# Moving steps of four engines' hand-written order in a fused two-layer encoder kernel

## The reference

```python
def encoder_layer(x, ...):
    hn = rmsnorm(x, g_pre_mix)
    proj = hn @ w_in                       # 1024 -> 3072
    # three token mixers on column groups of proj: dilated attention (q, k, v of 6 heads),
    # 2-D neighbourhood attention (4 heads), short gated convolution (384 channels)
    mixed = concat([y_dil, y_na, y_conv]) @ w_out
    x = x + rmsnorm(mixed, g_post_mix)
    hf = rmsnorm(x, g_pre_ffn)
    f = (silu(hf @ w_gate) * (hf @ w_up)) @ w_down      # 1024 -> 2816 -> 1024
    return x + rmsnorm(f, g_post_ffn)
# rmsnorm(x, g) = x * rsqrt(mean(x * x) + eps) * g
```

## Time and profile before

| | us |
|---|---|
| three runs, median | 3261.06 (3260.49 to 3262.88) |
| profiled execution, own time | 3261.06 |
| its span, first to last instruction | 3259.3 |
| TensorE busy | 3194.7 (98%) |
| VectorE busy | 1508.6 (46%) |
| ScalarE busy | 936.4 (29%) |
| GpSimd busy | 917.5 (28%) |
| mean granted TensorE clock | 0.993 of full speed |

### The profile page before, as it was taken

The page is one execution under the profiler, slowest core; times in us unless marked ns, Lnnn a source line. Parts: engine busy times, 40 slices in busy tenths (PEclk is TensorE's granted clock), DMA queues, the critical chain, the costliest instruction groups (busy, mean ns, idle before and its releaser), DMA issues.

```text
span 3259.3 us, 42970 instructions
## 1 busy us (share of the span) xinstructions
PE 3194.7 (98%) x17564; PEld 2726.9 (84%) x17564; DVE 1508.6 (46%) x3067; ACT 936.4 (29%) x1814; POOL 917.5 (28%) x653
## 2 busy tenths in 40 slices
PE   9999999999999999999999999999999999999997
PEld 8888887888888888888788888878888888888886
DVE  6766657253333333323687666562523333333336
ACT  5433444341111111111344344444411111111112
POOL 2111113553222222222342121135622222222223
PEclk9999999999999999999999999999999999999998
DMA  3111002131111111111321110121211111111112
GB/s 145 51 50 49 28 28 85 75 130 52 40 39 39 40 38 34 40 39 33 135 81 43 52 47 29 46 90 71 110 58 39 33 39 39 39 39 39 40 52 104
DMA packets 50483, 184.29 MB, mean 57 GB/s; under 512 B 8048, under 2 KB 11760, under 8 KB 46832
## 3 DMA queue, kind: packets, MB, share of 16 engines
q1 hardware_dynamic: 47984, 173.68, 15.7%
q10 hardware_dynamic: 2304, 7.87, 0.6%
HBM read 144.81 MB, written 28.84 MB: 53 GB/s over the span
## 4 chain that ended last, share of the span: by engine, by line
PE 88%; DVE 8%; issue 1%; ACT 1%; DMA 1%; POOL 0%; SPq 0%; DVEq 0%; POOLq 0%; ACTq 0%
PE PS L1783 26%; PE PS L1785 26%; PE PS L1784 25%; PE PS L1935 3%; PE PS L1904 3%; PE PS L1919 2%; DVE PT L1544 1%; DVE XL L1379 1%; DVE ACC L1372 1%; DVE ACC L1375 1%; PE PS L1820 1%; DVE YO L1375 1%; DVE YO L1372 1%; PE PS L1879 0%; ACT PT L1087 0%
## 5 line engine op out<-in xcount | busy, mean ns | idle before, releaser
L1783 PE MATMUL PS<-XH,WH 128*128 128x512 f32 (+1 forms) x3648 | 1325.7, 363 | 14.8 <-DVE XL L1379 4.4
L1785 PE MATMUL PS<-XH,WL 128*128 128x512 f32 (+1 forms) x3648 | 1299.9, 356 | 0.0
L1784 PE MATMUL PS<-XL,WH 128*128 128x512 f32 (+1 forms) x3648 | 1298.9, 356 | 0.0
L1783 PEld LDWEIGHTS PS<-XH,WH 128*128 128x128 f32 x3648 | 692.3, 190 | 138.9 <-issue 21.2
L1785 PEld LDWEIGHTS PS<-XH,WL 128*128 128x128 f32 x3648 | 692.3, 190 | 100.7
L1784 PEld LDWEIGHTS PS<-XL,WH 128*128 128x128 f32 x3648 | 692.9, 190 | 92.0
L808 POOL TENSOR_TENSOR WL<-RAW,WH 128x1024 fp32r<-128x1024 f32 x193 | 460.8, 2407 | 367.8 <-ACT WH L987 362.8
L831 POOL TENSOR_TENSOR SG<-SG,RS 128x512 f32<-128x512 f32 x132 | 147.2, 1115 | 994.5 <-ACT SG L1126 994.5
L1614 DVE TENSOR_TENSOR ACC<-ACC,PS 128x512 f32<-128x512 f32 (+1 forms) x480 | 286.4, 599 | 246.6 <-PE PS L1785 245.4
L1783 PE MATMUL PS<-HH,WH 128*128 128x512 f32 (+1 forms) x1056 | 379.3, 359 | 5.4 <-DVE ACC L1614 3.1
L1785 PE MATMUL PS<-HH,WL 128*128 128x512 f32 (+1 forms) x1056 | 378.9, 359 | 0.0
(11 more groups left out here) (123 smaller groups left out, 3019.5 us busy)
## 6 DMA issues: line engine op xcount, KB each, us to landing
RAW<-w_in SPq DMA_DIRECT2D x48, 512.0 KB, 3.5
RAW<-w_gate SPq DMA_DIRECT2D x44, 512.0 KB, 3.4
RAW<-w_up SPq DMA_DIRECT2D x44, 512.0 KB, 3.5
RAW<-w_down SPq DMA_DIRECT2D x44, 512.0 KB, 3.8
X<-parked SPq DMA_DIRECT2D x6, 2048.0 KB, 7.3
RAW<-w_out SPq DMA_DIRECT2D x16, 512.0 KB, 4.4
parked<-YO SPq DMA_DIRECT2D x4, 2048.0 KB, 6.6
mixed<-YB ACTq DMA_DIRECT2D x8, 640.0 KB, 2.9
```

The costliest lines, as they stand in the source:

```text
L1783: nc.tensor.matmul(out, wh, xh, start=first, stop=False)
L1784: nc.tensor.matmul(out, wh, xl, start=False, stop=False)
L1785: return nc.tensor.matmul(out, wl, xh, start=False, stop=last)
```

## The change

It moves instructions within the orders of four engines and adds or removes none:

- ScalarE, start: the high parts of the second and third weight (q, v) are made after the sixth and the eighth `first_high` of chunk 0 instead of both after the eighth.
- TensorE, start of layer 0: the sum of the input's chunk 1 is taken in the middle of the group q1 instead of after it.
- FFN stage 0, both layers: VectorE does all steps of chunk 2 before `hidden(L, 0, 0)` and `gate(L, 1, 0)`; ScalarE does all `new_high` of chunk 2 before `hidden_high(L, 0, 0)` and `silu(L, 1, 0)`, and `hidden_high(L, 0, 1)` goes between the sixth and the seventh square of chunk 2; GpSimd does `scaled_gate(L, 0, 1)` after the fifth tile's add (k = 4) of chunk 2 instead of after all.
- FFN last stage: VectorE puts three steps of chunk 0 (k = 3, 4, 5), not two (3, 4), between the accumulations of down chunk 1; it does no step of chunk 1 before `hidden(L, f + 1, 2)` (three or two before), and in the last layer four of them before the accumulations of down chunk 2. ScalarE follows with its `new_high` in layer 0.

```diff
@@ gpsimd
                 scaled_gate(L, 1, 0)
-                for k in range(KT):
+                for k in range(5):
                     add(e, "x", 2, k)
                 scaled_gate(L, 0, 1)
+                for k in range(5, KT):
+                    add(e, "x", 2, k)
                 invert(e, "x", 2)
@@ scalar
             for k in range(KT):
                 first_high(0, k)
-            high((0, "q", 0))
-            high((0, "v", 0))
+                if k in (5, 7):
+                    high((0, "q" if k == 5 else "v", 0))
...
                         square_new(e, 1, squared)
                         squared += 1
-                    if k == 4:
-                        hidden_high(L, 0, 0)
-                        silu(L, 1, 0)
+                hidden_high(L, 0, 0)
+                silu(L, 1, 0)
                 mean(e, "x", 1)
                 hidden_high(L, 1, 0)
                 keep(e, "x", 1)
                 for k in range(3):
                     square_new(e, 2, k)
                 silu(L, 0, 1)
-                for k in range(3, KT):
+                for k in range(3, 6):
                     square_new(e, 2, k)
                 hidden_high(L, 0, 1)
+                for k in range(6, KT):
+                    square_new(e, 2, k)
...
                 for k in range(KT):
                     square_acc(L, 1, k)
-                    if more_layers and k in (1, 4):
-                        new_high(e, 0, 3 + k // 4)
+                    if more_layers and k in (1, 3, 5):
+                        new_high(e, 0, 3 + k // 2)
...
                 if more_layers:
-                    new_high(e, 0, 5)
                     new_high(e, 0, 6)
...
                     high((L + 1, "q", 0))
-                    new_high(e, 1, 0)
-                    new_high(e, 1, 1)
                 hidden_high(L, f + 1, 2)
                 if more_layers:
                     high((L + 1, "v", 0))
-                    for k in range(2, KT):
+                    for k in range(KT):
                         new_high(e, 1, k)
@@ vector
                 gate(L, 0, 0)
-                for k in range(5):
+                for k in range(KT + 1):
                     step(e, 2, k)
                 hidden(L, 0, 0)
                 gate(L, 1, 0)
-                for k in range(5, KT + 1):
-                    step(e, 2, k)
                 hidden(L, 1, 0)
...
                     accumulate(L, END, 1, k)
-                    if k in (1, 4):
-                        step(e, 0, 3 + k // 4)
+                    if k in (1, 3, 5):
+                        step(e, 0, 3 + k // 2)
                 hidden(L, f, 2)
-                for k in range(5, KT + 1):
+                for k in range(6, KT + 1):
                     step(e, 0, k)
                 gate(L, f + 1, 2)
-                early = 3 if more_layers else 2
-                for k in range(early):
-                    step(e, 1, k)
                 hidden(L, f + 1, 2)
                 if more_layers:
-                    for k in range(early, KT + 1):
+                    for k in range(KT + 1):
                         step(e, 1, k)
...
                 else:
+                    for k in range(4):
+                        step(e, 1, k)
                     for k in range(KT):
                         accumulate(L, END, 2, k)
                         if k in (2, 5):
-                            step(e, 1, 2 + k // 3)
-                    for k in range(4, KT):
+                            step(e, 1, 4 + k // 3)
+                    for k in range(6, KT):
                         step(e, 1, k)
@@ tensor
-                    first_projection(L, "q", 1)
-                    sum_squares(e, "x", 1)
+                    first_projection(L, "q", 1, total=(e, "x", 1))
                     first_projection(L, "v", 1, (e, "x", 1))
```

## The result

The changed kernel takes 3281.01 us (median of four, 3279.85 to 3283.94) against 3260.77 us for the kernel before: a ratio of 1.0062, interval 1.0045 to 1.008, so 15 to 26 us slower. The forecast was 3278.0, range 3266 to 3284. The profiled execution took 3280.36 us (span 3278.6), 19.3 us more than that of before. One later kernel, with the last stage alone moved, was profiled in an execution at 0.85 of the full clock (3495.8 us), so its trace is not read and that run does not enter the ratio.

A forecast was written before the change was run, and what follows sets the result against it. The prediction took TensorE, busy 98% of the span, as the bound. Its terms, 0.75 + 1.8 + 9.4 + 3.4 + 1.5 + 0 = 16.85 us, on 3261.06 us gave 3278 us, range 3266 to 3284.

The forecast's parts named there:

- What bounds the kernel: Whole kernel: TensorE, busy 98% of the span, sets the time; moved instructions count only through its waits.
- The start, +0.75: Start: ScalarE waits for q's load, VectorE's last XL and weight splits come later, TensorE's second group starts 0.75 us later.
- The sum of chunk 1, +1.8: Input's chunk 1: the earlier sum waits 1.95 us for VectorE's last add; the next sum comes 1.8 us later.
- Stage 0, 2 x 4.7: FFN stage 0, both layers: late HF, spread and sum of chunk 2 cost 4.7 us a layer.
- HF's wait: Stage 0: ten instructions before HF, two meeting a GpSimd add, take 6.4 us; TensorE waits 2.2 us.
- The spread's wait of 1.2: Stage 0: chunk 1's mean comes late behind `silu(L, 1, 0)`, so TensorE waits 1.2 us more for the spread.
- The rival without collisions: Stage 0: VectorE's steps meet no GpSimd add, 2.5 us a layer, no clock loss: 3270 us; chance 0.13.
- The clock, +3.4: Start and stage 0 of either layer: new waits lower TensorE's clock in two of three places, 1.7 us each.
- Last stage, layer 0, +1.5: Layer 0's last stage: a third step delays the sum 3 us, of which 1.5 is given back later.
- Last stage, layer 1, 0: Layer 1's last stage: one step less for VectorE, as much more pause: 0 us, bounds -1.0 and +1.4.

The follow-up runs named there:

- the first half alone: VectorE's steps and ScalarE's `new_high` of chunk 2 moved ahead of `hidden` and `hidden_high` in stage 0, against the kernel before: 3267.92 us, ratio 1.0021.
- the kernel with thin adds: Only stage 0's steps and `new_high` moved, and GpSimd's seven chunk 1 adds cut to 4 of 512 columns, against the kernel before: 3260.89 us, ratio 1.0.

## Why the prediction was right

- **What bounds the kernel**: right. VectorE, ScalarE and GpSimd have the instructions of before; TensorE's waits and its clock make up the 19.3 us.
- **The start, +0.75**: right in that ScalarE waits for q's load and VectorE's XL come late, but size and place were off. The term was worked out from a load that landed at 11.1 us, the earliest of thirteen landings seen; from 12.2 it costs 1.8 us (beyond the bound of 1.0), from 12.9 with a lowered clock 3.9. And it counted the late XL only for VectorE's weight splits, on which the second group starts; TensorE itself stood for them already inside the first group (2.14 us, 1.06 with the start alone). "The load lands earlier in other runs" was the wrong side to bound.
- **The sum of chunk 1, +1.8**: right, place and size (a wait of 1.76, +1.9 in the trace).
- **Stage 0, 2 x 4.7**: right. HF's wait was 2.15 and 2.17 (2.2 forecast); in layer 0 two of the moved ten instructions met an add, as counted, and the ten took 6.42 us (6.4). The spread's wait of 1.2 was 0.85 in the first half alone, and hidden by the clock in the whole. The sum followed `keep` by 8.1 us as counted and was awaited 1.27 and 1.53 us (1.9 forecast). The rival without collisions is near what the kernel with thin adds shows: its HF was not only in time but early, as five older collisions were gone too, and VectorE's half of the stage cost nothing.
- **The clock, +3.4**: its cause is shown for stage 0 (filling the waits removes it), its size off. I took two of three places; in the profiled execution it fell in all three and in stage 0 twice a layer. Before, nine stretches at 1.2 GHz of 1.7 us lost work each can be counted in the trace (besides the last microseconds), after thirteen (six new ones in the start and in stage 0, one in layer 1's last stage, one less at 44 us and two less in layer 0's last stage): a balance of 6.8 us. What a stretch costs isn't always 1.7 us: behind the next wait part of it vanishes.
- **Last stage, layer 0, +1.5**: right in sign and mechanism (late at the sum by 2.5 us in the changed kernel and by 3.8 with layer 0's moves alone, 3 forecast, and most of it given back), +0.4 and +1.4 net in the two traces.
- **Last stage, layer 1, 0**: this step failed. It held that "VectorE's total work to the end is one step less and its pauses are as much more". The four steps took the 5.6 us forecast, but TensorE's wait of 3.46 us for the bank pushed the down groups, with them the last sum and `keep`, and VectorE, which before worked from 3238 us to the end without a pause, stood 1.76 us for it. The end was shared by both engines: +3.1 us in the trace, and with layer 1's moves alone +3.0 in the trace and 1.6 to 7.5 us in the times. The bound of +1.4 was too low.
- **Attention of layer 1**, no term: -1.6 us. The profile of before has a wait of 1.54 us for PT at 2185 us, which five of the thirteen profiled executions show, at much the same place, while in the others, the kernel after among them, it is 0.3 to 0.6 us. As kernels with and without moved instructions are in both lots, it seems to belong to the execution, not to the change.

The sum was 2.4 us low against the profiled execution, and the forecast 3.0 us low against the median: start and end 3.2 and 3.1 too low, stage 0 with its clock 0.5 too high, the last stage of layer 0 and the attention of both layers 3.3 too high. That these errors partly cancelled was luck; that stage 0 carries most of the time was read rightly.

## What to carry to other kernels

Count moved instructions at the duration that they have beside the neighbour engine's work in their new place, not at their own. Where a bank or buffer turns among three, look for what stands ahead of its first reader: a pause there can hold up both engines, and a count of one engine's work misses it. And on a kernel that TensorE bounds, a wait that can't be removed may still be worth filling with matmuls (2 to 8 us here in the last stages), but little where another wait stands behind it (stage 0). Before calling a clock stretch the result of an edit, compare several executions: here one followed the same wait of 0.9 us in eight executions of ten.

## What the runs showed of the hardware

- The same wait doesn't always lower the clock. Behind the unfilled wait of 0.9 us at 45 to 47 us it fell in eight of ten profiled executions. With the steps alone moved, stage 0 had waits for HF of 2.15 us in layer 0 and 2.17 in layer 1; the windows around read 1.00 and 0.97. The Trainium skill, "TensorE: Matmul & The Clock Gate", section "What's actually happening", has the clock set by how busy TensorE has been of late; that extra matmuls of no use keep it up, 0.97 and 0.94 to 1.00, agrees.
- It also falls where TensorE reports no pause: behind the 24 one-column matmuls at 3222 us, window 0.86 with 12.00 of 12 us busy.
- A load of 512 KB issued at 3.5 us, the seventh transfer of its queue, landed between 11.1 and 13.0 us in thirteen executions.
- A VectorE instruction on two operands in SBUF takes three times as long beside a GpSimd add (1.40 to 1.56 against 0.42 to 0.48 us at 256 columns), whichever of a step's three instructions it is.
